# Attention in two stages of a two-block transformer kernel: scores three units ahead, turns issued ahead of values, projections two heads ahead

## The reference

```python
def mla_mixer(u, ...):                       # latent attention: 16 heads, 512 tokens
    q = (rmsnorm_2(q_lat, q_norm_w) @ w_q_up)   # 384 -> 16 x (64 + 32)
    kv = (rmsnorm_2(kv_lat, kv_norm_w) @ w_kv_up)  # 256 -> 16 x (64 + 64)
    q_rope = apply_rope_2(q_rope, cos, sin)
    sc = q_nope @ k_nope.T + q_rope @ k_rope.T
    mask = k_chunk[None, :] <= q_chunk[:, None]    # chunks of 64
    p = softmax(sc * scale)
    return p @ v
...
def memory_attention(h, mem_h, wq, wk, wv, wo):  # 4 heads of 256, 256 memory tokens
    q, k, v = h @ wq, mem_h @ wk, mem_h @ wv
    p = softmax(q @ k.T * 256 ** -0.5)
    return (p @ v) @ wo
```

## Time and profile before

| | us |
|---|---|
| median of three runs | 3173.03 (3171.05 to 3174.96) |
| profiled execution, its own time | 3177.18 |
| its span | 3175.4 |
| mean granted TensorE clock | 0.878 |

### The profile page before, as it was taken

The page is one execution under the profiler, slowest core; times in us unless marked ns, Lnnn a source line. Parts: engine busy times, 40 slices in busy tenths (PEclk is TensorE's granted clock), DMA queues, the critical chain, the costliest instruction groups (busy, mean ns, idle before and its releaser), DMA issues. The chain is left out here.

```text
span 3175.4 us, 45114 instructions
## 1 busy us (share of the span) xinstructions
PE 2747.0 (87%) x17888; PEld 1969.3 (62%) x17888; DVE 1519.7 (48%) x2489; ACT 1087.4 (34%) x2032; POOL 309.8 (10%) x528
## 2 busy tenths in 40 slices
PE   6849997799999899868999999777777879889998
PEld 6737885578888666546444764565545468674445
DVE  4463334565325444545743455345343153458753
ACT  3323332333223333424322433212444244443322
POOL 0122221320023200014002300000000000000000
PEclk9959997889999899869999999555777789899999
DMA  4200000022232111101322222000000023013222
GB/s 156 93 0 1 2 2 1 2 105 99 88 107 69 40 41 47 54 1 56 120 94 105 80 107 73 27 0 14 1 34 18 36 101 139 27 54 125 89 90 82
DMA packets 29393, 189.02 MB, mean 60 GB/s; under 512 B 3136, under 2 KB 5440, under 8 KB 8192
## 3 DMA queue, kind: packets, MB, share of 16 engines
q1 hardware_dynamic: 28672, 184.29, 15.9%
q10 hardware_dynamic: 512, 1.85, 0.2%
HBM read 184.03 MB, written 2.10 MB: 59 GB/s over the span
## 5 line engine op out<-in xcount | busy, mean ns | idle before, releaser
L417 DVE SCALAR_TENSOR_TENSOR wsp<-raw_w,wsp 128x2048 f16<-128x2048 f32 (+2 forms) x180 | 398.9, 2216 | 248.1 <-ACT wsp L406 240.4
L392 PE MATMUL ps<-hn,wsp 128*128 128x512 f16 x1968 | 428.1, 381 | 4.4 <-DVEq L239 4.4
L387 PE MATMUL ps<-hn,wsp 128*128 128x256 f16 (+1 forms) x2976 | 360.5, 285 | 45.4 <-DVEq L239 15.2
L406 ACT ACTIVATE wsp<-raw_w 128x2048 f16<-128x2048 f32 (+2 forms) x180 | 326.8, 1816 | 118.0 <-PE ps L390 48.2
L387 PEld LDWEIGHTS ps<-hn,wsp 128*128 128x128 f16 x2976 | 300.6, 102 | 102.5 <-POOL hn L833 16.6
L392 PE MATMUL ps<-big,wsp 128*128 128x512 f16 (+1 forms) x1740 | 355.7, 368 | 5.8 <-DVE big L380 4.2
L390 PE MATMUL ps<-hn,wsp 128*128 128x264 f16 x2880 | 339.5, 282 | 7.3 <-DVE hn L659 7.3
L392 PEld LDWEIGHTS ps<-hn,wsp 128*128 128x128 f16 x1968 | 193.1, 98 | 238.5 <-DVEq L239 4.7
L390 PEld LDWEIGHTS ps<-hn,wsp 128*128 128x128 f16 x2880 | 287.5, 100 | 55.7 <-issue 7.5
L392 PEld LDWEIGHTS ps<-big,wsp 128*128 128x128 f16 x1740 | 175.4, 101 | 180.6 <-issue 23.1
L387 PE MATMUL ps<-big,wsp 128*128 128x256 f16 (+1 forms) x1800 | 208.2, 278 | 21.2 <-DVEq L239 15.0
(11 more groups left out here) (366 smaller groups left out, 3608.6 us busy)
## 6 DMA issues: line engine op xcount, KB each, us to landing
raw_w<-slabs SPq DMA_DIRECT2D x162, 1024.0 KB, 5.0
raw_w<-slabs SPq DMA_DIRECT2D x10, 512.0 KB, 5.2
raw_w<-slabs SPq DMA_DIRECT2D x8, 384.0 KB, 4.8
h<-xin SPq DMA_DIRECT2D x1, 2112.0 KB, 7.6
out<-hn SPq DMA_DIRECT2D x8, 256.0 KB, 2.5
big<-memx ACTq DMA_DIRECT2D x1, 1024.0 KB, 4.9
sml<-small SPq DMA_DIRECT2D x1, 768.0 KB, 10.5
cst<-consts SPq DMA_DIRECT2D x1, 738.0 KB, 9.0
```

The costliest lines, as they stand in the source:

```text
L387: mm = L.eng.matmul(ps[:rows, b, 0:T // 2], lhsT, rhs[:, z, :], start=first, stop=last)
L392: mm = L.eng.matmul(two(ps[:rows, b, 0:T]), lhsT, rhs, start=first, stop=last)
L406: L.fin(L.eng.activation(wsp[:, n % NW, 0, lo:hi], raw_w[:, q % 2, 0:hi - lo], ACT.Copy, scale=WSCALE), "hi")
L417: L.fin(L.eng.scalar_tensor_tensor(wsp[:, n % NW, 1, lo:hi], raw_w[:, q % 2, 0:hi - lo], WSCALE, wsp[:, n % NW, 0, lo:hi], ALU.mult, ALU.s ...
```

## The change

Latent stage: scores are issued three units ahead instead of two, and the turn of unit n+1 ahead of the values of unit n, on TensorE, and the copies likewise on ScalarE. `Pm` gets a third buffer. A function `four_banks` drains the accumulators and lets `acc_slot` hand out banks 0, 2, 4, 3 for the length of the stage. The values use one place of bank 7 instead of two, so values n wait for output copy n-1 (before: n-2). `head_up` is divided: keys of head hd+2 are projected at the end of the head's third iteration, the query of hd+2 at the end of its fourth; the first two heads' queries come before the loop. The second four values projections move to the ends of iterations 28 to 31. Splits go by single halves, at the ends of iterations 20, 24, 25, 51, 52, 56 and 57.

Memory stage: scores three ahead (with banks 0, 2, 4), turn n+1 ahead of values n.

```diff
-        SPLITS = (23, 26, 55, 58)
+        SPLITS = (20, 24, 25, 51, 52, 56, 57)
...
+            if four and four[0] <= n and (len(four) < 2 or n < four[1]):
+                return (0, 2, 4, 3)[(n - four[0]) % 4]
             return 2 * (n % 3)
...
-            L.take("acc_free", max(0, n - 2 - L.taken.get("acc_free", 0)))
+            ahead = 3 if len(four) == 1 else 2
+            L.take("acc_free", max(0, n - ahead - L.taken.get("acc_free", 0)))
...
-        Pm = ml_c(2, SEQ)
+        Pm = [sq[:, 0, 0:SEQ], sq[:, 1, 0:SEQ], ml_c(SEQ)]
...
             for n in range(64):
                 hd, i = n // 4, n % 4
-                if i == 1 and hd + 1 < 16:
-                    head_up(hd + 1)
-                if 29 <= n < 33:
-                    values_up(n - 29)
-                if n + 2 < 64:
-                    mla_scores(n + 2)
+                if n + 3 < 64:
+                    mla_scores(n + 3)
+                if n + 1 < 64:
+                    turn_pe(L, n + 1, (n + 1) % 4 + 1)
                 pe.wait_ge(sem("vm"), (0 if hd < 8 else 4) + i + 1)
                 values_pe(L, n, i + 1, None)
-                if n + 1 < 64:
-                    turn_pe(L, n + 1, (n + 1) % 4 + 1)
-                if i == 2 and hd % 2 == 0 and hd:
+                if n == 26:
+                    slabs_up()
+                if i == 1 and hd % 2 == 0 and hd:
                     pair_out(hd // 2 - 1)
+                if i == 2 and hd % 2 == 0 and hd + 2 < 16:
+                    key_up(hd + 2)
+                if i == 3 and hd + 2 < 16:
+                    query_up(hd + 2)
+                if 28 <= n < 32:
+                    values_up(n - 28)
...
             for n in range(16):
-                if n + 2 < 16:
-                    mem_scores(n + 2)
-                values_pe(L, 64 + n, 2, (2 * (n // 4), 2 * (n // 4) + 1))
+                if n + 3 < 16:
+                    mem_scores(n + 3)
                 if n + 1 < 16:
                     turn_pe(L, 65 + n, 2)
+                values_pe(L, 64 + n, 2, (2 * (n // 4), 2 * (n // 4) + 1))
...
-            if n >= 2:
-                pe.wait_ge(sem("out_read"), n - 1)
-            at = 256 * (n % 2)
+            if n >= 1:
+                pe.wait_ge(sem("out_read"), n)
...
             for n in range(64):
                 hd, i = n // 4, n % 4
-                if i == 1 and hd + 1 < 16:
-                    head_dve(hd + 1)
-                if n + 2 < 64:
-                    unit_max(n + 2, ((n + 2) % 4 + 1) * P, sq_, acc_next())
+                if n + 3 < 64:
+                    unit_max(n + 3, ((n + 3) % 4 + 1) * P, sq_, acc_next())
                 if n + 1 < 64:
                     unit_sum(n + 1)
-                if i == 2 and hd % 2 == 0 and hd:
+                if i == 1 and hd % 2 == 0 and hd:
                     pair_dve(hd // 2 - 1)
+                if i == 3 and hd + 2 < 16:
+                    head_dve(hd + 2)
                 if n in SPLITS:
-                    split_lo(L, dcnt)
+                    split_lo_part(L, dcnt)
...
             for n in range(64, 80):
-                if n + 2 < 80:
-                    unit_max(n + 2, MEM, 1.0 / 16, acc_next())
+                if n + 3 < 80:
+                    unit_max(n + 3, MEM, 1.0 / 16, acc_next())
                 if n + 1 < 80:
                     unit_norm(n + 1, MEM)
```

More of the change, by code:

```diff
@@ L393, in mm_split @@
             return mm
-        def split_hi(L, cnt):
[L397 to L407, removed]
@@ L409, in split_lo, with split_hi_part @@
-        def split_lo(L, cnt):
[L411 to L419, removed]
+        def split_hi_part(L, cnt):
+            if not cnt.get("rest"):
+                n = cnt["split"] = cnt.get("split", -1) + 1
+                if n >= len(plan):
+                    return
+                if n >= NW:
+                    done, count = freed[n - NW]
+                    L.eng.wait_ge(sem(done), count)
+                cnt["rest"] = halves_of(n)
+            n = cnt["split"]
+            lo, hi = cnt["rest"].pop(0)
+            q = cnt["half"] = cnt.get("half", -1) + 1
+            L.eng.wait_ge(sem(f"half{q % 2}"), 16 * (q // 2 + 1))
+            L.fin(L.eng.activation(wsp[:, n % NW, 0, lo:hi], raw_w[:, q % 2, 0:hi - lo], ACT.Copy,
+                                   scale=WSCALE), "hi")
@@ new lines, in split_hi, with split_lo_part @@
+        def split_hi(L, cnt):
+            split_hi_part(L, cnt)
+            while cnt.get("rest"):
+                split_hi_part(L, cnt)
+        def split_lo_part(L, cnt):
+            if not cnt.get("rest"):
+                n = cnt["split"] = cnt.get("split", -1) + 1
+                if n >= len(plan):
+                    return
+                cnt["rest"] = halves_of(n)
+            n = cnt["split"]
+            lo, hi = cnt["rest"].pop(0)
+            q = cnt["half"] = cnt.get("half", -1) + 1
+            L.take("hi")
+            L.fin(L.eng.scalar_tensor_tensor(wsp[:, n % NW, 1, lo:hi], raw_w[:, q % 2, 0:hi - lo], WSCALE,
+                                             wsp[:, n % NW, 0, lo:hi], ALU.mult, ALU.subtract), "half_used")
+            if not cnt["rest"]:
+                L.tell("split")
@@ L1129, in head_up, with key_up @@
                     freed[ups["n"][1]] = ("acc_full", L.made["acc_full"])
[L1130 to L1136, removed]
+            def key_up(hd):
+                j = hd % 8
+                b = acc_open(L, cnt)
+                for k in range(2):
+                    mm = mm_split(L, b, [z[:, k, j * 64:j * 64 + P] for z in ups["w"][0]], zt(27 + k), SEQ,
+                                  k == 0, k == 1)
+                L.put(mm, "acc_full")
+                if j == 6:
+                    freed[ups["n"][0]] = ("acc_full", L.made["acc_full"])
             def values_up(i):
@@ L1171, in second_pe @@
             L.take("krope")
-            head_up(0)
+            four_banks(L, cnt)
+            slabs_up()
+            query_up(0)
+            key_up(0)
+            query_up(1)
             for i in range(4):
                 values_up(i)
-            mla_scores(0)
-            mla_scores(1)
+            for n in range(3):
+                mla_scores(n)
             turn_pe(L, 0, 1)
@@ L1213, in mem_scores @@
                 L.put(mm, "acc_full")
-            mem_scores(0)
-            mem_scores(1)
+            for n in range(3):
+                mem_scores(n)
             st_drain(L, cnt)
@@ L1829, in second_act @@
                 L.tell("vm")
-            unit_exp(64, MEM, 1.0 / 16.0)
-            unit_exp(65, MEM, 1.0 / 16.0)
+            for n in range(64, 67):
+                unit_exp(n, MEM, 1.0 / 16.0)
             unit_turn(64, 2)
@@ L2302, in second_dve @@
             head_dve(0)
-            unit_max(0, P, sq_, acc_next())
-            unit_max(1, 2 * P, sq_, acc_next())
+            head_dve(1)
+            for n in range(3):
+                unit_max(n, (n + 1) * P, sq_, acc_next())
             unit_sum(0)
```

91 lines of the change are left out of this document (52 added, 39 removed).

## The result

The changed kernel takes **3182.78 us** (median of six; 3179.88 to 3187.44) against 3172.97 for the kernel before in the same measurement: a ratio of 1.0032, 95% interval 1.0019 to 1.0045. It is slower by 0.2 to 0.3%. The forecast was 3180.5 us, from 3148 to 3204, slower. Its profiled execution took 3180.88 us (span 3179.1), 3.7 more than that of before (3177.18). Two executions, one of e10 (5334.54 us) and one of the kernel before beside it (4640.64 us), count as slow, and the ratios leave them out.

A forecast was written before the change was run, and what follows sets the result against it. Bound: TensorE waiting on a chain over three engines, with a lowered clock in the latent stage. Latent -6.5 and memory +14 give +7.5 on the profiled 3177.18, so 3184.7; against the runs' median 3180.5 us, range 3148 to 3204.

The forecast's parts named there:

- Memory stage, +14: Memory stage: turns wait for normalisation queued behind a maximum, values come after; period 3.71 us instead of 2.66, +14 us.
- Latent heads, -8.4: Latent stage: shorter waits gain 0 to 1.1 us per head, 0.6 taken, for 14 heads that project: -8.4 us.
- the chain: Latent change of head: projection, rotation (ends 3.16), maximum, exponential (4.07), turn copy (5.03), output copy (5.43), values (5.8 us).
- Splits, +4: Latent stage: seven single halves cost about 21 us against 17 for the splits before: +4 us.
- values projections, +1.6: Latent stage: of four iterations with second values projections, two lie in waits, the others on the path: +1.6 us (0 to 3).
- the head without a projection, -6: Latent stage: head 14 now projects nothing, losing 3.7 us of waits and nine matmuls: -6 us.
- +2.3 for nine matmuls: Ahead of the latent loop: the second query's projection, nine matmuls at 0.23 us, uncovered: +2.3 us (0 to 4.0).
- The latent sum: Latent stage: heads, head without projection, query ahead of the loop, values projections and splits together: -6.5 us.
- The first, full clock in the latent stage: Latent stage: heads run at full clock nearly throughout, 13.35 us each; total 3148 us; chance 0.20.
- The third: Latent stage: every split costs 4.5 us and heads gain nothing; latent +6, total 3193 us; chance 0.13.
- the fourth: Memory stage: scores run so far ahead that maxima are done early; memory 0, total 3166.5 us; chance 0.10.
- The second, memory at half clock: Memory stage: clock falls to half, period 5.65 us, 39 us instead of 13.6; total 3206 us; chance 0.17.

The follow-up runs named there:

- e10: The kernel before with ScalarE's exponential moved last in the latent stage, still two units ahead with two buffers: 3119.6 us, 0.9831 of the kernel before.
- e1: The changed kernel with VectorE's normalisation ahead of the maximum in the memory stage: 3167.27 us, 0.9972 of the kernel before.
- e5: The changed kernel with ScalarE's exponential behind the turn and output copies in the latent stage: 3139.06 us, 0.9891 of the kernel before.
- e4: The changed kernel with whole slabs split at 20, 24, 51 and 56 instead of single halves: 3175.65 us, 1.0002 of the kernel before.
- e0: The changed kernel measured again, unedited, as base for later runs: 3180.5 us, 1.0024 of the kernel before.
- e9: e8 with the query projected at the end of a head's second iteration, its rotation one iteration later, and splits moved: 3079.7 us, 0.9704 of the kernel before.
- e7: The changed kernel with VectorE's query rotation behind the maximum of 512 keys in the latent stage: 3166.17 us, 0.9982 of the kernel before.
- e8: The changed kernel with the edits of e1 and e5 together: 3117.28 us, 0.9828 of the kernel before.
- e12: e10 with the next head's projections, copies and rotation one iteration earlier: 3121.89 us, 0.9838 of the kernel before.

## Why the prediction was right, point by point

**Memory stage, +14.** Right in mechanism, place and nearly in size: 47.1 to 59.1 us, +12.0. The step mis-sized is the last term of the period. I let 1.05 us pass from the values' start to the next scores, from the weight loads; measured are 0.89 (2704.44 to 2705.33), so the period is 3.56 and not 3.71. The other two terms stand: scores to turn 2.39, turn to values 0.28. The clock of 1.00 that I took held in the loop. There are twelve such periods and not thirteen, since the first two turns are 2.64 us apart in both kernels; the stage's entry and its last values took 3.0 us more where I had 1.0, and its last units gained 1.7 instead of 0.7, so these small terms nearly cancel. e1 shows the cause by removing it.

**Latent heads, -8.4.** The eight heads with neither splits nor second values projections (1 to 4, 8 to 11) take 15.7 us on the mean, from 14.8 to 16.5; the same eight took 16.1 before. That is 0.4 a head, inside 0 to 1.1 and under the 0.6 that I took. The times of the chain, 3.16, 4.07, 5.03, 5.43 and 5.8 in the text, are 3.19, 4.08, 4.98, 5.38 and 5.84 in the profile. But I read this chain as given and took the middle of 0 and 1.1; I did not ask which of its links was only an order of issue. e5 and e10 show that ScalarE's was one.

**Splits, +4, values projections, +1.6, and the head without a projection, -6.** By the output copies heads 5 to 7 take 55.7 us (before 58.2), heads 13 and 14 40.6 (before 41.6), and with head 12, in which a split now lies too, 57.8 (before 57.8). So these six heads gain 2.5 us in all, what the chain gives at 0.4 a head, and the +5.6 for splits and values projections was not there (e4's pairs, at nearly the same places, are still 2 us shorter). The head that no longer has a projection's chain is the first one by the output copies. It gains 3.3 us in this profile, and 1.1 in e0's, and the last head gains 4.1 in both: 7.4 or 5.1 against my 6. Ahead of the loop the latent stage takes 3.5 us longer to its first scores, and 3.9 to its first output copy, where I had +2.3 for nine matmuls at full clock; they took 0.39 us each. The latent sum was forecast as -6.5 and is -9.2 (289.8 to 280.6): terms that were wrong by up to 5.6 us each and lie on both sides.

**Rivals.** The first, full clock in the latent stage, came nowhere near: 0.76. Nothing here prices it: e9, at 0.88, has a latent stage 94 us shorter than that of before, but with waits removed as well. The third is excluded by the latent stage's 9 us (by its own prices it was at least +7.4 and not +6), the fourth by the memory stage's period. The second, memory at half clock, was not in the changed kernel's profile but was in that of e7, for two periods:

```profile
2686.74 0.69 PE L1287 MATMUL ps<-cst,wk 128*128 128x128 f32 x2 [1.36 <-DVE wk L2343]
...
2687.22 1.92 PE L1304 MATMUL ps<-wk,big 128*128 128x128 f32 x8
...
2688.93 1.91 PE L1257 MATMUL ps<-big 128*128 128x256 f32 x4
...
2692.21 0.69 PE L1287 MATMUL ps<-cst,wk 128*128 128x128 f32 x2 [1.37 <-DVE wk L2343]
...
2697.68 0.44 PE L1287 MATMUL ps<-cst,wk 128*128 128x128 f32 x2 [1.36 <-DVE wk L2343]
```

```profile
2687.00:2690.00 3.00, 3.00 (x13) 2.82 (x13) 0.00 (x0) 0.90 (x3) 0.00 (x0) 0.50 0.00 0
2700.00:2710.00 10.00, 5.69 (x39) 4.79 (x40) 3.26 (x12) 3.87 (x13) 0.00 (x0) 1.00 0.00 1
```

5.47 us from turn to turn (2686.74 to 2692.21), against the 5.65 that I had worked out; then the clock came back and stayed at 1.00 with TensorE busy 5.69 of 10 us. So it cost some 4 us in the execution that it hit. By what the Trainium skill reports (TensorE: Matmul & The Clock Gate, "A second HAM failure mode: psum-queue depth-cycling") frequent short idles would have kept the stage swinging. The traces don't bear that out for this stage: apart from these two periods of e7 its loop ran at 1.00, with 1.36 us idle in each 3.56.

**Sum.** 3180.5 against 3182.78: the profiled pair differs by 3.7 us where 7.5 were forecast (memory 2 less, latent gain 2.7 more, and +1.0 in stretches that the forecast left alone), the medians by 9.8 and 7.2 in two measurements. The forecast's sum was 3.8 us above the profiled pair and 2.3 below the medians, since the profiled execution of before stands 4.2 us above its median and that of the changed kernel 1.9 below. So coming within 2.3 us is luck, and so is that the latent terms added up; the cause in the memory stage and most of its size are not.

## What to carry to other kernels

Running further ahead does not help while an engine's own list puts the far-ahead step in front of the near one that others wait for. Issue on each engine first what is next needed (copies, normalisation), and last what is furthest ahead. In the latent stage that was worth 41 to 54 us, and the whole change of that stage without it 9; in the memory stage it turned +12 into -4. When an issue order is changed on one engine, follow the wait back to the queue in which its releaser stands, and change both. A deeper pipeline gained nothing before that (e8 against e10); that it pays afterwards is what e9 against e12 suggests.

## What was not expected of the hardware

Removing waits from TensorE also shortened the matmuls that were left, as the granted clock rose. By the windows of each run's latent stage (first scores to last pair), TensorE's idle time goes from 71.9 us in the changed kernel to 43.4 in e5 and 25.5 in e9, and its busy time, for the same 896 instructions, from 193.3 to 180.5 and 158.8, as the clock goes from 0.76 to 0.80 and 0.88. So of the 81 us between the first and the last, 46 are waits and 35 are matmuls that took less time. None of my sums had that second part. And in the memory stage's loop TensorE was busy 62% of its time (21.97 of 35.61 us in the changed kernel) with the clock at 1.00 throughout, while in the latent stage 66% in a stretch of 3.4 us was followed by half clock; what tells the two apart was not tried.
